# A decoder pair on one core: the feed-forward layers' second projection by Strassen's scheme

## The reference, cut to what matters

```python
hn = rms_norm(h, ln_mlp[layer])                                          # [512, 1024]
h = h + jnp.square(jax.nn.relu(hn @ w_mlp1[layer])) @ w_mlp2[layer]      # 1024 -> 4096 -> 1024
gate = jax.nn.sigmoid(rms_norm(h, ln_ple[layer]) @ w_ple_gate[layer])
h = h + (p[layer] @ w_ple_proj[layer]) * gate
```

## Time and profile before

| | before |
|---|---|
| median of 3 runs | 2019.27 us (2018.52 to 2019.58) |
| the profiled execution, first to last instruction | 2018.7 us, 0.6 us under the median; the profile has no other time for this execution |
| granted TensorE clock | 1.000 of full speed |
| TensorE matmul busy | 1965.9 us, 97% |
| VectorE, ScalarE busy | 1067.5 us (53%), 892.7 us (44%) |
| GpSimd busy | 227.9 us (11%) |

### The profile page before, as it was taken

The page is one execution under the profiler, slowest core; times in us unless marked ns, Lnnn a source line. Parts: engine busy times, 40 slices in busy tenths (PEclk is TensorE's granted clock), DMA queues, the critical chain, the costliest instruction groups (busy, mean ns, idle before and its releaser), DMA issues.

```text
span 2018.7 us, 27316 instructions
## 1 busy us (share of the span) xinstructions
PE 1965.9 (97%) x11149; PEld 1587.5 (79%) x11149; DVE 1067.5 (53%) x1707; ACT 892.7 (44%) x1661; POOL 227.9 (11%) x232
## 2 busy tenths in 40 slices
PE   7999999999999999999999999999999999999998
PEld 6778888888888788656888888878888888967667
DVE  5576565344434552666643433356625765555764
ACT  5572354322324563666432323247534452355663
POOL 1011000000000000342000000000000033233440
PEclk9999999999999999999999999999999999999999
DMA  5221123332321322111323323313331245711001
GB/s 153 78 76 52 36 66 99 104 104 84 105 101 68 103 93 84 63 42 43 94 85 103 105 84 105 104 63 102 101 100 60 66 134 159 190 42 42 3 1 73
DMA packets 125090, 170.13 MB, mean 84 GB/s; under 512 B 9675, under 2 KB 85975, under 8 KB 124967
## 3 DMA queue, kind: packets, MB, share of 16 engines
q1 hardware_dynamic: 117046, 151.13, 23.4%
q0 software_dynamic: 5568, 14.64, 2.6%
q10 hardware_dynamic: 2352, 2.62, 0.4%
HBM read 158.42 MB, written 2.10 MB: 80 GB/s over the span
## 4 chain that ended last, share of the span: by engine, by line
PE 77%; DVE 10%; ACT 8%; issue 3%; DMA 1%; POOL 0%; SPq 0%; DVEq 0%; ACTq 0%
PE PSUM L526 60%; PE PSUM L564 5%; PE PSUM L534 5%; DVE WL L413 2%; DVE AR L413 2%; ACT AR L430 2%; ACT XN L430 2%; DVE AR L421 2%; PE PSUM L541 1%; ACT WH L492 1%; ACT TM L430 1%; DVE ST L2912 1%; PE PSUM L2616 1%; PE PSUM L2665 1%; PE PSUM L2637 1%
## 5 line engine op out<-in xcount | busy, mean ns | idle before, releaser
L413 DVE TENSOR_TENSOR WL<-RAW,WH 128x1024 fp32r<-128x1024 f32 (+2 forms) x284 | 346.7, 1222 | 369.3 <-ACT WH L492 368.7
L492 ACT CAST WH<-RAW 128x1024 fp32r<-128x1024 f32 (+2 forms) x284 | 293.6, 1036 | 365.8 <-PE PSUM L526 356.7
L526 PE MATMUL PSUM<-XH,WH 128*128 128x512 f32 (+3 forms) x1120 | 399.8, 369 | 5.1 <-ACT XH L734 1.7
L526 PE MATMUL PSUM<-XH,WL 128*128 128x512 f32 (+3 forms) x1120 | 392.6, 363 | 1.3 <-DVE WL L413 1.3
L526 PE MATMUL PSUM<-XL,WH 128*128 128x512 f32 (+3 forms) x1120 | 392.1, 363 | 0.0
L526 PE MATMUL PSUM<-WH,HP 128*128 128x512 f32 x1024 | 317.7, 390 | 1.9 <-DVE WL L413 1.9
L526 PE MATMUL PSUM<-WH,XH 128*128 128x512 f32 (+2 forms) x608 | 238.1, 392 | 3.5 <-DVE WL L413 3.5
L526 PEld LDWEIGHTS PSUM<-XH,WH 128*128 128x128 f32 (+2 forms) x1120 | 204.6, 187 | 43.9 <-issue 7.5
L526 PEld LDWEIGHTS PSUM<-XL,WH 128*128 128x128 f32 (+2 forms) x1120 | 204.9, 187 | 35.6 <-issue 2.9
L526 PEld LDWEIGHTS PSUM<-XH,WL 128*128 128x128 f32 (+2 forms) x1120 | 204.8, 187 | 35.2 <-DVE WL L413 1.7
L526 PE MATMUL PSUM<-WH,XL 128*128 128x512 f32 (+2 forms) x608 | 230.9, 380 | 0.0
(11 more groups left out here) (238 smaller groups left out, 2474.4 us busy)
## 6 DMA issues: line engine op xcount, KB each, us to landing
RAW<-in_w_mlp_dram SPq DMA_DIRECT2D x64, 1024.0 KB, 5.2
RAW<-in_nsa_w_in_dram SPq DMA_DIRECT2D x13, 1024.0 KB, 6.4
RAW<-in_w_in_e_dram SPq DMA_DIRECT2D x12, 1024.0 KB, 5.4
RAW<-in_w_qkv_o_dram SPq DMA_DIRECT2D x12, 1024.0 KB, 5.1
RAW<-in_gla_w_in_dram SPq DMA_DIRECT2D x12, 1024.0 KB, 5.2
RAW<-in_w_ple_gate_dram SPq DMA_DIRECT2D x8, 1024.0 KB, 5.0
RAW<-in_w_out_e_dram SPq DMA_DIRECT2D x4, 1024.0 KB, 5.0
RAW<-in_w_out_o_dram SPq DMA_DIRECT2D x4, 1024.0 KB, 5.0
```

The source lines that it names most:

```text
L413: return x.do.tensor_tensor(o, a, b, op)
L492: a.do.copy(hi, r).then_inc(*up("w_hi", "w_hi", j))
L526: m = p.do.matmul(o, l, r, start=start and i == 0, stop=stop and i == len(pairs) - 1)
```

## The change

The second projection of a quarter becomes Strassen's scheme in Winograd's form: tokens are cut in two halves, hidden features in even and odd tiles, output columns in two halves, and seven products of blocks (256 tokens by 512 features by 512 columns) replace eight. Each product is two weight parts and 24 matmuls. The weight blocks b11, b12, b21, b22 are loaded into four slots of AR beside the ring; GpSimd makes from them, in place, t1 = b12 - b11, t2 = b22 - t1, t3 = b22 - b12, t4 = b21 - t2 (128x1024 at a time), and from the hidden tiles four sums for each pair of tiles (128x256 each, into XN). Both kinds are split in high and low parts as all operands are: `sums_half` and `sums_rest` do it for the token sums, and the weight parts go through the ring of three. One bank gathers p1, p1 + p6, p1 + p6 + p7, and p1 + p6 + p7 + p4, and VectorE adds it to H after each, before TensorE goes on in it; so there are 14 adds for a quarter instead of 8. down(q) now follows up(q) at once, and HP has one buffer. At the end of the layer token tiles 2 and 3 are the last to finish, in columns 0 to 511, and turn 2 moves into the first half of `pv`. Some waits for small loads now wait for two of them.

```diff
-        def up(q):
-            F(I["w_mlp1"][i], 1024 * q, 1024 * q + 1024)
-
-        def down(q):
-            T(I["w_mlp2"][i], 0, 1024, 8 * q, 8 * q + 8)
-        up(0)
-        for q in range(1, 4):
-            up(q)
-            down(q - 1)
-        down(3)
+        def block(q, name):
+            r, c = int(name[1]) - 1, int(name[2]) - 1
+            plan.append((name, rows(I["w_mlp2"][i])[:, 8 * q + r:8 * q + 8:2, 512 * c:512 * c + 512], i, q))
+
+        for q in range(4):
+            F(I["w_mlp1"][i], 1024 * q, 1024 * q + 512)
+            block(q, "b11")
+            F(I["w_mlp1"][i], 1024 * q + 512, 1024 * q + 768)
+            block(q, "b12")
+            F(I["w_mlp1"][i], 1024 * q + 768, 1024 * q + 1024)
+            block(q, "b22")
+            block(q, "b21")
...
+BLOCKS = {"b11": 7, "b12": 8, "b21": 9, "b22": 11}
+OPERANDS = ("b11", "b21", "t1", "t2", "b22", "t3", "t4")
+STANDS_IN = {"t1": "b11", "t2": "b11", "t3": "b12", "t4": "b21"}
+A11, A12, A22, S1, S2, S3, S4 = range(7)
...
+PRODUCTS = [
+    Product("p1", A11, "b11", "x", None, (0, 0), False),
+    Product("p2", A12, "b21", "z", None, (0, 0), True),
+    Product("p5", S1, "t1", "y", None, (1, 1), False),
+    Product("p6", S2, "t2", "x", "p1", (0, 1), False),
+    Product("p3", S4, "b22", "y", "p5", (0, 1), True),
+    Product("p7", S3, "t3", "x", "p6", (1, 1), False),
+    Product("p4", A22, "t4", "x", "p7", (1, 0), True),
+]
...
-        out.extend((("hid", l, q, m), ("hid_lo", l, q, m)) for q in range(4) for m in range(8))
+        out.extend((("hid", l, q, m), ("sums_lo", l, q, m // 2)) for q in range(4) for m in range(8))
...
-        with nc.sbuf_tensor("HP", [128, 2, 2, 8, 512], FR) as HP:
+        with nc.sbuf_tensor("HP", [128, 7, 2, 4, 256], FR) as HP:
...
+            name, src, l, q = plan[u]
+            if q == 0:
+                s.wait_ge(*(at("op", 7) if l else at("hx", 3)))
+            elif name == "b11":
+                s.wait_ge(*at("w", operand_part["t2", l, q - 1, 1]))
+                s.wait_ge(*at("combined", "t4", l, q - 1, 1))
+            elif name == "b12":
+                s.wait_ge(*at("w", operand_part["t3", l, q - 1, 1]))
+            elif name == "b22":
+                s.wait_ge(*at("w", operand_part["b22", l, q - 1, 1]))
+            else:
+                s.wait_ge(*at("w", operand_part["t4", l, q - 1, 1]))
+            load(s, f"raw_{name}", ("raw", u), weights_of(name), src)
...
-                return ps.free("down", n // 4, 3, 1, t)
+                return ps.free("down", n // 4, 3, "xy"[t < 2], t % 2)
...
-                return ps.free("down", n // 4, 3, 0, t)
+                return ps.free("down", n // 4, 3, "z", t) if t < 2 else at("bank_read", n // 4, 3, "p7", t - 2)
...
+            def operand_ready(q, prod):
+                if prod.tokens == A11:
+                    p.wait_ge(*at("hid_lo", l, q, 6))
+                elif prod.tokens in (A12, A22):
+                    p.wait_ge(*at("hid_lo", l, q, 7))
+                else:
+                    p.wait_ge(*at("sums_lo", l, q, 3))
+
+            def quarter(q, prod, i, half, j, hi, lo):
+                job = ("down", l, q, prod.bank, i)
+                if prod.after is None and half == 0:
+                    ps.take(*job, keep=True)
+                    p.wait_ge(*ps.empty(*job))
+                if prod.after and half == 0:
+                    p.wait_ge(*at("bank_read", l, q, prod.after, i))
...
+            def down(q, mid):
+                for prod in PRODUCTS:
+                    operand_ready(q, prod)
+                    if prod.name in ("p7", "p4"):
+                        got = [part(p, "B") for _ in range(2)]
+                        order = [(i, half) for i in range(2) for half in range(2)]
+                    else:
+                        got = [None, None]
+                        order = [(i, half) for half in range(2) for i in range(2)]
+                    for i, half in order:
+                        if got[half] is None:
+                            got[half] = part(p, "B")
+                        j, hi, lo = got[half]
+                        p.wait_ge(*at("w", j))
+                        quarter(q, prod, i, half, j, hi, lo)
+                        if half and (prod.name, i) in mid:
+                            mid[prod.name, i]()
...
+            def sums_half(q, i):
+                a.wait_ge(*at("sums", l, q, i))
+                a.do.copy(HP[:, S1:S4 + 1, 0, i, :], sums(i)).then_inc(*up("sums_hi", "sums_hi", l, q, i))
...
+                    if q and m == 0:
+                        a.wait_ge(*ps.full("down", l, q - 1, "x", 1))
+                    if m and m % 2 == 0:
+                        sums_half(q, m // 2 - 1)
...
+            def down(q):
+                j = operand_part["b11", l, q, 0]
+                act_weights(a, j + 3)
+                sums_half(q, 3)
+                if q < 3:
+                    act_weights(a, j + 16)
+                    return
+                act_weights(a, j + 7)
+                act_half(a, n + 1, 0)
+                act_half(a, n + 1, 1)
+                act_weights(a, j + 12)
+                act_scale(a, n + 1, 0)
+                act_scale(a, n + 1, 1)
+                act_weights(a, j + 13)
+                act_half(a, n + 1, 2)
+                act_weights(a, j + 14)
+                act_half(a, n + 1, 3)
+                act_turn(a, n + 1, 0)
+                act_weights(a, j + 15)
+                act_scale(a, n + 1, 2)
+                act_turn(a, n + 1, 1)
+                act_weights(a, j + 16)
+                act_scale(a, n + 1, 3)
+                act_turn(a, n + 1, 2)
+                act_turn(a, n + 1, 3)
...
+            def sums_rest(q, i):
+                v.wait_ge(*at("sums_hi", l, q, i))
+                tt(v, HP[:, S1:S4 + 1, 1, i, :], sums(i), HP[:, S1:S4 + 1, 0, i, :].bitcast(F32), ALU.subtract).then_inc(
+                    *up("sums_lo", "sums_lo", l, q, i))
...
+                    if m and m % 2 == 0:
+                        sums_rest(q, m // 2 - 1)
...
+            def down(q):
+                j = operand_part["b11", l, q, 0]
+                dve_weights(v, j + 3)
+                sums_rest(q, 3)
+                for k in range(4):
+                    dve_weights(v, j + 4 + 2 * k)
+                    add(q, k, 0)
+                    add(q, k, 1)
+                    if q == 3 and k == 1:
+                        dve_half(v, n + 1, 0)
+                        dve_half(v, n + 1, 1)
+                    dve_weights(v, j + 5 + 2 * k)
+                if q < 3:
+                    dve_weights(v, j + 12)
+                    add(q, 4, 0)
+                    add(q, 4, 1)
+                    add(q, 5, 0)
+                    dve_weights(v, j + 13)
+                    add(q, 5, 1)
+                    dve_weights(v, j + 14)
+                    add(q, 6, 0)
+                    dve_weights(v, j + 15)
+                    add(q, 6, 1)
+                    dve_weights(v, j + 16)
                     return
-                for t in range(4):
-                    add(t)
-                    if q == 3:
-                        dve_half(v, n + 1, t)
-                if q < 3 or c == 0:
-                    dve_weights(v, j + 6)
+                add(q, 4, 0)
+                add(q, 4, 1)
+                dve_weights(v, j + 12)
+                dve_scale(v, n + 1, 0)
+                add(q, 5, 0)
+                dve_weights(v, j + 13)
+                dve_scale(v, n + 1, 1)
+                add(q, 5, 1)
+                dve_half(v, n + 1, 2)
+                dve_weights(v, j + 14)
+                add(q, 6, 0)
+                dve_gain(v, n + 1, 0)
+                dve_half(v, n + 1, 3)
+                dve_weights(v, j + 15)
+                dve_rest(v, n + 1, 0)
+                add(q, 6, 1)
+                dve_gain(v, n + 1, 1)
+                dve_scale(v, n + 1, 2)
+                dve_rest(v, n + 1, 1)
+                dve_weights(v, j + 16)
+                dve_gain(v, n + 1, 2)
+                dve_scale(v, n + 1, 3)
+                dve_rest(v, n + 1, 2)
+                dve_gain(v, n + 1, 3)
+                dve_rest(v, n + 1, 3)
...
+            def token_sums(q, i):
+                x, y, s = tm("hid", l, q, 2 * i), tm("hid", l, q, 2 * i + 1), sums(i)
+                first, second = slice(0, 256), slice(256, 512)
+                g.wait_ge(*at("hid_sq", l, q, 2 * i))
+                g.wait_ge(*at("hid_sq", l, q, 2 * i + 1))
+                if q or i >= 2:
+                    g.wait_ge(*at("sums_lo", l, q - (i < 2), (i + 2) % 4))
+                tt(g, s[:, 2, :], x[:, first], x[:, second], ALU.subtract)
+                step(g, tt(g, s[:, 0, :], y[:, second], x[:, second], ALU.add))
+                step(g, tt(g, s[:, 1, :], s[:, 0, :], x[:, first], ALU.subtract))
+                tt(g, s[:, 3, :], y[:, first], s[:, 1, :], ALU.subtract).then_inc(*up("sums", "sums", l, q, i))
+
+            def combine(q, name, i):
```

(75 more changed lines are left out.)

199 lines of the change are left out of this document (111 added, 88 removed).

## The result

The changed kernel takes 2059.36 us (median of 4 runs, 2058.18 to 2064.37) against 2019.42 us: a ratio of 1.0204 over the runs, with a 95% interval from 1.0190 to 1.0219 (the two medians alone give 1.0198). It is slower by 40 us, where 22 were forecast. That is at the very edge of the range that ends at 2060: the median lies 0.6 us inside it, 2019.27 x 1.0204 = 2060.5 us half a microsecond outside. The direction and the mechanism were those of the forecast, the size was not. The profiled execution spans 2062.6 us, the longest of the four (the other three span 2056.4, 2057.4 and 2057.6 us), so what follows is read from single quarters, and totals are taken from medians.

What follows compares the result with a forecast made beforehand. The prediction took TensorE's pace, 0.2267 us a matmul with nothing waited for, as the bound. It summed 2018.7 - 43.5 (matmuls) + 56 (stalls in quarters) + 9 (layer ends) = 2040.2, so 2041 us, range 1989 to 2060.

Steps and rivals of the forecast that it cites:

- Removed, 43.5 us: Second projection, 192 to 168 matmuls a quarter: 24 x 8 x 0.2267 = 43.5 us saved over all quarters.
- VectorE's and ScalarE's own additions cost nothing: Each quarter's extra casts, splits and adds, 16.4 us on VectorE and 10.5 on ScalarE, were expected to fit.
- The step that decides: GpSimd's operations and VectorE's two-SBUF-operand subtractions block each other and take turns: 7.0 us a quarter, 56 us in all.
- The price of a difference: A GpSimd difference of 128x1024 with two full inputs was taken at 2.35 us.
- the forecast's sign: Listed as showing the forecast right: GpSimd busy some 28 us a quarter more.
- Before p1, 2.9 us: Ahead of p1 each quarter, its last token part is ready late behind GpSimd's t1 turns: 2.9 us stall.
- Within the products, 4.1 us: In the seven products, turns make part 8 ready at 25.9 us where 21.8 is wanted: 4.1 us stall.
- A fourth quarter like the others: One steady quarter was followed and its 7.0 us of stall counted for all 8 quarters.
- End of each layer, 4.5 us: Turns behind p4, the late second half of pv and a late cast: 4.5 us a layer, 9 in all.
- VectorE's 35.5 us a quarter: VectorE's existing work in a quarter, 113.27 x 88.6/283 = 35.5 us, to which 16.4 us were added.
- The rival of turns that don't bind: GpSimd's differences mostly fall into VectorE's waits, at most 2 us a quarter: 1980 to 2001 us, chance 0.28.
- slower still: Rival: GpSimd's difference at 2.54 us and stalls shifting token sums 3 into the next turn: 2056 us, chance 0.13.

Runs made afterwards that it cites:

- e12: The changed kernel with all GpSimd additions cut to one column and the two layer-end moves of e6; 1978.15 us, ratio 0.9796.
- e2: The changed kernel with all GpSimd differences and token sums cut to one column, waits and order kept; 1989.53 us, ratio 0.9853.
- e8: The changed kernel with GpSimd's eight block differences a quarter cut to one column, token sums kept; 1987.54 us, ratio 0.9843.
- e1: The changed kernel with GpSimd's differences and token sums replaced by fills that read nothing, waits kept; 1990.22 us, ratio 0.9851.
- e11: The changed kernel with first norm halves of tiles 0 and 1 placed later in each layer's last quarter; 2059.54 us, ratio 1.0200.
- e6: The changed kernel with p4's last add moved earlier and the embedding product's first two banks emptied before the norm of tiles 2 and 3; 2051.64 us, 1.0157.
- e7: The kernel before the change with 64 extra GpSimd subtractions of 128x1024 on a buffer nothing reads; 2019.41 us, ratio 0.9999.
- e4: The changed kernel with 12 more matmuls of 512 columns ahead of p1 in each quarter; 2062.13 us, ratio 1.0211.
- e9: The changed kernel with only t1's two differences moved from GpSimd to VectorE; 2051.51 us, ratio 1.0166.

## Why the prediction was wrong in size

By medians the change is -43.5 (matmuls) + 2.3 (e12 against that) + 11.4 (e2 - e12, the two waits at the layer ends) + 69.8 (the change - e2, GpSimd's work) = 40.0 us; with e8 in place of e2, whose runs spread by 7 us, the last two terms are 9.4 and 71.8. The forecast had -43.5 + 9 + 56.

**The step that failed** is the size of the waits in that sum: 8 x 7.0 = 56 us within the quarters, where the medians give some 70, and 9 us at the layer ends, where they give 11.4 + 2.3 = 13.7. In the quarters 7.0 us was short for the plain ones (7.6 to 8.8) and far short for the fourth of each layer (14), which was taken to be like the others. The profiled execution has 50.0 us over in its six plain quarters and 25.0 in its two fourth ones (beyond the 1.7 that each has in e1), 75 us in all and some 5 us more than the medians; so how the 14 us above the forecast's 56 divide in a usual run is not settled.

- *Removed, 43.5 us:* right. e12 comes within 2.3 us of it.
- *VectorE's and ScalarE's own additions cost nothing:* right, e1 and e2.
- *The step that decides:* right as a mechanism. e1 takes the reading away and keeps GpSimd at work and the waits; the time falls by 69 us. It agrees with the rule of the Trainium skill that was named (SBUF — State Buffer, "Who interferes with whom"), also in that a GpSimd instruction that only writes does not block: e1's splits are at 1225 ns beside fills.
- *The price of a difference:* 2.41 us, for 2.35 in the sum; the Trainium skill's figure (GPSIMD Engine Reference, "Elementwise — side-by-side cycle accounting") would make an estimate of 2.25, 7% low. GpSimd is busy 40 us a quarter more, where the forecast's sign said some 28; its own prices make 8 x 2.35 + 16 x 0.73 = 30.5, and the rest is time in which GpSimd is blocked.
- *Before p1, 2.9 us:* 2.88 us in six quarters. In the first of each layer it is 1.89, and I took it as the others.
- *Within the products, 4.1 us:* it had part 8 ready 25.9 us after p1's start, for 21.8 wanted. In the quarter shown its split ends at 551.91, after 26.6 us, so the turns took 0.7 us more than in my sum. And p3, which uses it, starts only after 27.35 us: it goes on in bank y, and VectorE's add of p5 to that bank stands behind the split (551.83). **This edge, 0.7 us, was missing.** p3 is 5.6 us late, not 4.1, and the quarter lasts 46.71 us, 8.6 above 38.09, for 7.0. The quarters 0 to 2 lasted 7.6, 8.8 and 8.6 us too long.
- *A warning on reading such a delay off the idle times:* they are 1.66 + 0.52 + 1.23 + 0.97 = 4.4 us within the products and 7.1 with the one ahead of p1, 1.5 short of 8.6. The matmul ahead of a wait lasts 0.39 us at a pace of 0.23, so 0.16 us lie in it, and the first one behind it is followed at 0.30 to 0.34 us instead of 0.23. That is some 0.3 us for each of five waits.
- *A fourth quarter like the others:* wrong. It is 14.3 and 14.0 us over. Of this 1.7 are there without GpSimd's work (e1: turn 0 and a wait of 0.47 us). 2.3 come from `dve_half` behind GpSimd's t2 (the wait ahead of p6's second half is 3.5 us for 1.2), and 2.6 to 2.9 from the lower clock behind that wait, in the one profiled; the wait of 1.0 us ahead of p3 is gone there. How much of this the median holds is not settled, since e11 shortened it without a gain.
- *End of each layer, 4.5 us:* mis-sized. e2 has some 7 us a layer, 5.7 of them by e6's two moves (e2 against e12), which take away two waits: turn 1's second bank is that of p4, whose add stood behind a split and two low parts (3.0 us), which I had not seen, and the copy of `pv`'s banks (2.9 us), which I had at about 3. The clock fell behind them; from p4 to the end of `pv` it took 25.6 us in the first layer and 20.0 in the second, with 13.9 before.
- *A slip without effect:* VectorE's 35.5 us a quarter uses 88.6 us for a quarter; 384 matmuls at 0.2267 make 87.0, so 34.8 us.
- *The rival of turns that don't bind* had the better part of the average on its side, and was wrong: 0.28 was too much for it, beside three rows that showed the blocking. The rival *slower still* came within 4 us of the result with 2056, but by luck: its condition, 2.54 us for a difference, did not hold (2.41). The range's upper end should have held the case in which every term comes out at the high side.

## What to carry to other kernels

Before giving elementwise work to an idle GpSimd, count the VectorE instructions with two SBUF operands that it will meet, at the place where they are wanted fastest, not on the average over a stage: each meeting costs up to the whole duration of the other's instruction. Here a VectorE with a difference more in its own list (1.29 us) was far cheaper than the idle engine (2.41 us and a turn), and it made a scheme pay that lost 2%. When you forecast a delay, follow each product to all that it waits for, the bank as well as the operand, and go through the quarter that differs by itself. And one wait can lie in front of another: removing the one ahead of p1 gave 8 us, where that wait by itself costs 20.

## What the runs showed of the hardware that was not expected

- GpSimd's fills of 128x1024 take 0.96 us and leave VectorE's two-operand subtractions at 1225 ns; its subtraction makes them up to 3.42 us.
- A subtraction of 128x1024 on GpSimd takes 2.41 us with two different inputs, and 1.895 us on the mean where both inputs are the same buffer (e7, first layer).
- The granted clock fell from 2.4 to 1.2 GHz near the end of waits of TensorE (from 1 us ahead of it to 2 us behind), for 3.4 or 6.8 us, in some quarters and not in others of the same order; the longest wait ahead of such a fall was between 1.0 us (e4, e6) and 3.6 us (e9). Matmuls then follow each other at 0.427 us. Behind p1 this cost nothing, since the next wait grew shorter by as much (e4).
